# Turnings and scores side by side in the attention stages of a two-block transformer on one core

## The chip, the cores and the metric

The kernel runs on 1 core of one Trainium2 chip. The time is what the device takes for one launch, in microseconds; the median of 3 runs before the change is 2911.08 us (2909.06 to 2913.7). The profile is of one further execution.

## The reference

Two blocks work on 512 tokens of width 1024, all in float32. The first block has two layers, each with a feed-forward part, a "mix" part (a convolution beside an attention with forget gates), a cross-attention to a memory and a second feed-forward part. The second block has a differential attention layer and a "stick-breaking" attention layer. The change touches the three self-attentions:

```
# mix: 8 heads of 64, causal
s = q k^T * scale + c_q - c_k ;  p = softmax(where(mask, s, -inf)) ;  o = p v
# differential: 8 heads, each with two q, k pairs of 64 and one v of 128
a = softmax(q1 k1^T * scale) - lam * softmax(q2 k2^T * scale) ;  o = a v
# stick-breaking (last stage): 16 heads of 64
z = q k^T * scale ;  log_1mb = where(mask, log_sigmoid(-z), 0)
suffix = reverse_cumsum(log_1mb) - log_1mb
a = where(mask, exp(log_sigmoid(z) + suffix), 0) ;  o = a v
```

## The kernel before, in words

**Stages and products.** The program has ten stages in a row (`STAGES`): ffn1, mix, x, ffn2 twice, then diff and sb (the last stage). TensorE computes every projection as a float32 product in three matmuls of high and low halves (`mm3`, L1525 to L1527): low weight times high input, high times low, high times high. In the text one such matmul of 512 columns is called **a product**; a projection tile has 24 of them (8 blocks of the width, 3 matmuls each). Weights come by DMA into RAW. ScalarE copies the high half to WH (L1872, L1875 for weights with a gain), VectorE subtracts to get the low half WL (L2255). In the last stage GpSimd first multiplies the raw weights by a gain (L2783).

**A row.** The attention works on pairs of heads. A pair t has four rows of 128 queries, numbered n = 4t to 4t+3; row i of a pair sees 128, 256, 384 or 512 keys. A row passes through these steps:

- **scores** (`pair_scores`, L1770): six matmuls of 64 rows of the array, into PSUM banks 4 and 5. In the mix two more of 40 rows (L1785) add the forget term.
- **weights of the row.** In mix and diff VectorE masks (L2423, L2617) and takes the maximum (L2425, L2619), ScalarE takes the exponential with its sum (L2003, L2129), then VectorE and in the mix GpSimd scale the row. In the last stage ScalarE takes two sigmoids (L2170, L2171), VectorE scans the products along the keys (L2701) and corrects the diagonal (L2705), and GpSimd multiplies the two (L2889).
- **turning** (`turn`, L1531): TensorE transposes blocks of 128 by 128 into bank 6 (diff) or banks 6 and 7 (mix, last). One row takes i+1 transposes in diff and 2(i+1) in the other two. ScalarE copies the high half out (L2139, L2179) and VectorE takes the low half (L2644, L2711), which frees the banks for the next turning.
- **values** (`bpv`, L1811 and L1812 in mix and last): after four turned rows, products with v.

**What sets the order.** The class `Plan` writes one list of steps, and each engine works through the entries that concern it, strictly in that order, with waits on semaphores. The attention of four rows is a side stream (`att`) that is woven into the main stream of projection matmuls (`weave`). Each `yield` in `att` ends one step. `stream(g, rate)` says how many steps are taken per unit of main work; two units are one `mm3` of 512 columns, so three products. A turning belongs to row n-2 (mix, diff) or n-3 (last) and stands in `att` just before the scores of row n, with a `yield` after each. Steps that follow up on another engine are put off with `later(k, ...)` by k units of main work, and `due(...)` puts them into the list at once where something needs them. The slots of WH and WL and a clock of planned steps (`PACE`) decide where in the list the low halves of the weights (`low`) stand.

**Groups in the last stage.** For t = 2 to 7 the loop in `stick` weaves four rows into the q and k tiles of the next pair. For odd t a value tile is added. So groups alternate: long ones (80 units of main work) and short ones (48).

**Other steps that the text names.** `gb` (L2723) multiplies the gate, which frees the gate's bank; `gy` (L2730) applies the gate to the output; `gl` (L2736) takes the output's low half. In diff `dn` (L1726) sums squares of q or k with 8 small matmuls and waits for two passes on ScalarE (`dsq`, L2097 and L2102); `dlo` (L2608) writes the low half of q or k; `dol` (L2669) writes the low half of the output.

Of the kernel before, what the change touches and what calls it, by code (L numbers as in the profile page):

```python
# [108 lines left out]
class Plan:  # L109
# [372 lines left out]
    def mix(self, s):  # L482
# [15 lines left out]
        def qk(w, t):  # L498
            b = self.take()
            yield from self.tile(((s, f"{w}{t}"), 0), b)  # L500
            self.give(b, "bql", (s, w, t))
            self.heads_in(s, w, t)
# [22 lines left out]
        def values_of(t, hh):  # L525
            b = self.take()
            self.bank_of[s, t, hh] = b
            self.add("mpv", (s, t, hh), "pv", "pvx")
            self.give(b, "mpl", (s, t, hh))
            self.later(3, "mps", (s, t, hh), "pvs")  # L530
            self.later(6, "mpq", (s, t, hh), "ysq", *(("yacc",) if t and hh else ()), "yh")
            self.later(10, "mpl", (s, t, hh), "yl")

        def att(n0, n1):

            for n in range(n0, n1):
                m = n - 2
                if m > 0 and m % 4 == 0:
                    self.due("btl", (s, m - 1))
                    for i in range(2):  # L540
                        self.due("evl", (((s, f"v{(m - 4) // 8}"), 0), i))
                    for hh in range(2):
                        values_of(m // 4 - 1, hh)
                        yield
                if 0 <= m < 16:
                    self.due("mn", (s, m))
                    self.due("btl", (s, m - 1))
                    self.later(4, "btl", (s, m), "pl")
                    self.add("bt", (s, m), "ptr", "ph")
                    yield  # L550
                if n < 16:
                    for w in "qk":
                        self.due("bql", (s, w, n // 4))
                    self.due("mn", (s, n - 1))
                    self.add("ms", (s, n), "score", "nbias", "exps")
                    self.later(10, "mn", (s, n), "fac", "gprob")
                    yield
# [44 lines left out]
        self.drain(self.flow(self.values(s, 0)))  # L602
        self.drain(self.flow(conv("c", 0)))
        self.add("ctr", (s,), "ctr", "cq")
        side = self.stream(att(0, 4), 6.5 / 64)
        self.weave(self.flow(self.chain(conv("v", 0), conv("b", 0), qk("q", 1), qk("k", 1))), side)
        for m in (1, 2):
            self.finish(side)
            side = self.stream(att(4 * m, 4 * m + 4), 10.5 / 80)
            self.weave(self.flow(self.chain(conv("c", m), conv("v", m), conv("b", m), qk("q", m + 1), qk("k", m + 1))), side)  # L610
        self.finish(side)
        side = self.stream(att(12, 16), 10.5 / 80)
        self.weave(self.flow(self.chain(self.values(s, 1), conv("c", 3), conv("v", 3), conv("b", 3))), side)
        self.finish(side)
        self.own_banks(0, 1, 2, 3, 4, 5)
# [1 line left out]
        side = self.stream(att(16, 19), 4.5 / 44)  # L617
# [178 lines left out]
    def diff(self, s):  # L796
# [52 lines left out]
        def att(n0, n1):  # L849

            for n in range(n0, n1):
                m = n - 2
                if m > 0 and m % 4 == 0:
                    self.due("dtl", (s, m - 1))
                    for i in range(2):
                        self.due("evl", (((s, f"v{(m - 4) // 8}"), 0), i))
                    values_of(m // 4 - 1)
                    yield
                if 0 <= m < 32:
                    self.due("dc", (s, m))  # L860
                    self.due("dtl", (s, m - 1))
                    self.add("dt", (s, m), "ptr", "ph")
                    self.later(4, "dtl", (s, m), "pl")
                    yield
                if n < 32:
                    for w in "qk":
                        self.due("dlo", (w, n // 4))
                    self.due("dc", (s, n - 1))
                    self.add("ds", (s, n), "score", "nbias", "exps")
                    self.later(6, "dc", (s, n), "prob")  # L870
                    yield
# [33 lines left out]
        for t in range(7):  # L905
            main = [qk("k", t + 1), qk("q", t + 1)]
            if t in (2, 4):
                main.append(self.values(s, t // 2 + 1))
            main.append(gated(t))
            side = self.stream(att(4 * t, 4 * t + 4), 9.4 / (80 if t in (2, 4) else 48))  # L910
            self.weave(self.flow(self.chain(*main)), side)
            self.finish(side)
        out = []
# [15 lines left out]
            for c, b in ((0, 6), (1, self.take())):  # L929
                yield from self.tile(out[2], b, c, range(7))  # L930

        side = self.stream(att(28, 33), 10.4 / 33)
        self.weave(self.flow(opening()), side)
        self.finish(side)
        side = self.stream(att(33, 36), 2.4 / 28)
# [116 lines left out]
    def stick(self, s):  # L1052
# [37 lines left out]
        def att(n0, n1):  # L1090

            for n in range(n0, n1):
                m = n - 3
                if m > 0 and m % 4 == 0:
                    self.due("btl", (s, m - 1))
                    for i in range(2):
                        self.due("evl", (((s, f"v{(m - 4) // 8}"), 0), i))
                    for hh in range(2):
                        values_of(m // 4 - 1, hh)
                        yield  # L1100
                if 0 <= m < 32:
                    self.due("bmul", (s, m))
                    self.due("btl", (s, m - 1))
                    self.add("bt", (s, m), "ptr", "ph")
                    self.later(5, "btl", (s, m), "pl")
                    yield
                if n < 32:
                    for w in "qk":
                        self.due("bql", (s, w, n // 4))
                    self.due("bmul", (s, n - 1))  # L1110
                    self.add("bs", (s, n), "score", "exps", "sbe")
                    self.later(5, "bsc", (s, n), "fac", "bel")
                    self.later(5, "bmul", (s, n), "gprob")
                    yield
# [15 lines left out]
        self.add("mq", (s,), "mask", "zero", "tri")  # L1130
        for w, t in (("q", 0), ("k", 0), ("q", 1)):
            self.heads_in(s, w, t)
        side = self.stream(att(0, 4), 6 / 64)
        self.weave(self.flow(self.chain(qk("k", 1), self.values(s, 0), gated(0))), side)
        for t in range(2, 8):
            self.finish(side)
            main = [qk("q", t), qk("k", t)]
            if t % 2:
                main.append(self.values(s, t // 2))
            if t < 7:  # L1140
                main.append(gated(t - 1))
            side = self.stream(att(4 * t - 4, 4 * t), 10.5 / (32 + (32 if t % 2 else 0) + (16 if t < 7 else 0)))
            self.weave(self.flow(self.chain(*main)), side)
        self.finish(side)
        banks = (0, 4, 6, 2)
# [4 lines left out]
            yield from self.chain(gated(6), gated(7))  # L1150
            yield from self.mm(out[0], range(0, 6))

        side = self.stream(att(28, 33), 13 / 56)
        self.weave(self.flow(opening()), side)
        self.finish(side)
        side = self.stream(att(33, 36), 6 / 20)
# [1767 lines left out]
```

## Time and profile before

| | |
|---|---|
| runs | 2909.06, 2911.08, 2913.7 us |
| the profiled execution | 2911.05 us, of it the span of instructions 2909.2 us |
| TensorE matmul busy | 2843.3 us (98%) |
| TensorE weight load busy | 2363.5 us (81%) |
| VectorE busy | 1676.3 us (58%) |
| ScalarE busy | 1092.2 us (38%) |
| GpSimd busy | 397.3 us (14%) |
| mean granted TensorE clock | 0.995 |
| chain of work that ended last | TensorE 82%, VectorE 10%, ScalarE 3%, issue 3% |

Matmuls overlap: one of 512 columns is shown with 0.39 us, and the next one starts 0.23 us after it. So the busy share of TensorE says little of how much time could be won; the starts of matmuls, one behind the other, say it. A number in square brackets at the end of a row is how long the engine sat idle before it, and who ended that.

### The profile page before, as it was taken

The page shows a single profiled execution, that of the slowest core. Times are in us where ns is not written, and L with a number is a line of the kernel's source. Part 1 is how long each engine was busy: PE and PEld are TensorE (multiplying, and loading weights), DVE is VectorE, ACT ScalarE, POOL GpSimd, SP SyncE. Part 2 cuts the span into 40 slices and gives each one's busy share as a digit, 9 for nine tenths or more (in the row PEclk, how much of TensorE's full clock was granted, in tenths as well). Part 3 has the DMA queues.
Part 4 walks back from the last instruction along what each step waited for, and adds up shares of the span by engine and source line. Part 5 has one row for each costly group of instructions (what it writes and reads, how often), then busy time and mean ns, then how long its engine had stood idle before and what let it go on. Part 6 is the DMA issues. An engine that isn't in the chain of part 4 may idle for free.

```text
span 2909.2 us, 34967 instructions
## 1 busy us (share of the span) xinstructions
PE 2843.3 (98%) x14241; PEld 2363.5 (81%) x14241; DVE 1676.3 (58%) x2400; ACT 1092.2 (38%) x1699; POOL 397.3 (14%) x263
## 2 busy tenths in 40 slices
PE   8999999999999999999999999999999899899988
PEld 7888887888888888888887889888888787678777
DVE  5554357675464533555247776555533677768884
ACT  4322244554332322323234454422222444444442
POOL 2000111110100001000011220100001322154430
PEclk9999999999999999999999999999999999999999
DMA  4332332243233233332323233233323222131211
GB/s 141 101 95 94 95 88 73 66 127 106 87 94 97 88 101 98 101 95 87 105 71 92 68 108 118 80 109 95 101 91 98 70 64 69 47 88 59 72 59 51
DMA packets 302240, 258.08 MB, mean 89 GB/s; under 512 B 11367, under 2 KB 299904, under 8 KB 302080
## 3 DMA queue, kind: packets, MB, share of 16 engines
q1 hardware_dynamic: 300704, 254.76, 28.7%
q8 instruction: 113, 1.85, 0.3%
q10 hardware_dynamic: 1024, 1.05, 0.2%
q14 instruction: 47, 0.39, 0.0%
q0 software_dynamic: 352, 0.03, 0.0%
HBM read 252.66 MB, written 2.10 MB: 88 GB/s over the span
## 4 chain that ended last, share of the span: by engine, by line
PE 82%; DVE 10%; ACT 3%; issue 3%; POOL 2%; DMA 1%; ACTq 0%; SPq 0%; POOLq 0%; DVEq 0%
PE PS L1525 26%; PE PS L1527 25%; PE PS L1526 25%; DVE WL L2255 3%; PE PS L1531 2%; PE PS L1770 1%; DVE AF L2701 1%; DVE SM L2619 1%; ACT AF L2129 0%; PE PS L1623 0%; PE PS L1812 0%; PE PS L1811 0%; DVE AR L2711 0%; ACT WH L1872 0%; POOL SM L2869 0%
## 5 line engine op out<-in xcount | busy, mean ns | idle before, releaser
L2255 DVE TENSOR_TENSOR WL<-RAW,WH 128x1024 fp32r<-128x1024 f32 x480 | 617.9, 1293 | 572.9 <-ACT WH L1872 572.6
L1525 PE MATMUL PS<-XH,WL 128*128 128x512 f32 x2256 | 904.4, 401 | 2.9 <-DVE XL L2265 2.9
L1527 PE MATMUL PS<-XH,WH 128*128 128x512 f32 x2256 | 883.3, 392 | 0.0
L1526 PE MATMUL PS<-XL,WH 128*128 128x512 f32 x2256 | 882.1, 391 | 0.0
L1872 ACT ACTIVATE WH<-RAW 128x1024 fp32r<-128x1024 f32 x448 | 465.4, 1044 | 1005.9 <-PE PS L1527 994.6
L1525 PEld LDWEIGHTS PS<-XH,WL 128*128 128x128 f32 x2256 | 425.8, 189 | 101.5 <-issue 12.7
L1527 PEld LDWEIGHTS PS<-XH,WH 128*128 128x128 f32 x2256 | 425.2, 188 | 91.5
L1526 PEld LDWEIGHTS PS<-XL,WH 128*128 128x128 f32 x2256 | 426.3, 189 | 81.1
L1525 PE MATMUL PS<-AR,WL 128*128 128x512 f32 (+1 forms) x1216 | 465.3, 383 | 7.3 <-DVE SC L2599 3.5
L1527 PE MATMUL PS<-AR,WH 128*128 128x512 f32 (+1 forms) x1216 | 460.7, 379 | 0.0
L1526 PE MATMUL PS<-AR,WH 128*128 128x512 f32 (+1 forms) x1216 | 460.6, 379 | 0.0
L2805 POOL TENSOR_TENSOR SC<-SC 128x512 f32<-128x512 f32 x70 | 117.5, 1678 | 1619.3 <-ACT SC L1897 1614.7
L1525 PEld LDWEIGHTS PS<-AR,WL 128*128 128x128 f32 x1216 | 229.4, 189 | 52.0 <-issue 9.2
L1527 PEld LDWEIGHTS PS<-AR,WH 128*128 128x128 f32 x1216 | 229.2, 188 | 43.1
L1526 PEld LDWEIGHTS PS<-AR,WH 128*128 128x128 f32 x1216 | 229.4, 189 | 41.0
L1525 PE MATMUL PS<-WH,XL 128*128 128x256 f32 x384 | 113.3, 295 | 0.8 <-DVE AR L2693 0.8
L2324 DVE TENSOR_TENSOR AF<-PS,RB 128x512 f32<-128x512 f32 x88 | 60.4, 687 | 85.9 <-PE PS L1527 85.9
L1526 PE MATMUL PS<-WL,XH 128*128 128x256 f32 x384 | 109.1, 284 | 0.0
L1527 PE MATMUL PS<-WH,XH 128*128 128x256 f32 x384 | 109.0, 284 | 0.0
L2337 DVE TENSOR_TENSOR AR<-AF,AR 128x512 fp32r<-128x512 f32 x88 | 60.9, 692 | 61.7 <-ACT AR L1934 61.7
L2318 DVE TENSOR_TENSOR SC<-PS,RB 128x512 f32<-128x512 f32 x88 | 60.1, 687 | 59.1 <-PE PS L1527 45.6
L1934 ACT ACTIVATE AR<-AF 128x512 fp32r<-128x512 f32 x88 | 55.3, 628 | 98.5 <-DVE AF L2332 98.5
(259 smaller groups left out, 3000.0 us busy)
## 6 DMA issues: line engine op xcount, KB each, us to landing
RAW<-in_w_ffn_gu_dram SPq DMA_DIRECT2D x176, 512.0 KB, 3.5
RAW<-in_w_ffn_down_dram SPq DMA_DIRECT2D x80, 512.0 KB, 3.4
RAW<-in_w_mix_in_dram SPq DMA_DIRECT2D x48, 512.0 KB, 4.0
RAW<-in_w_xkv_dram SPq DMA_DIRECT2D x32, 512.0 KB, 3.4
RAW<-in_a_w_in_dram SPq DMA_DIRECT2D x32, 512.0 KB, 4.2
RAW<-in_w_mix_out_dram SPq DMA_DIRECT2D x16, 512.0 KB, 3.4
RAW<-in_w_xq_dram SPq DMA_DIRECT2D x16, 512.0 KB, 4.1
RAW<-in_w_xo_dram SPq DMA_DIRECT2D x16, 512.0 KB, 3.4
```

The lines of the kernel that those rows point to most:

```text
L1525: pe.matmul(o, ll, rh, start=start, stop=False, skip_group_check=skip)
L1526: pe.matmul(o, lh, rl, start=False, stop=False, skip_group_check=skip)
L1527: return pe.matmul(o, lh, rh, start=False, stop=stop, skip_group_check=skip)
L1531: t = pe.transpose(PS[b][:, i * 128:(i + 1) * 128], src[:, i * 128:(i + 1) * 128], ID)
L1770: w = pe.matmul(PS[4 + hh][:, 0:N], QK[r, q, qs], QK[r, k, 0:N], start=q == sl + 1, stop=last and q == sl and k == sl + 2)
L1872: act.activation(h, src, ACT.Copy).then_inc(sg["wh"].up(n))
L1934: act.activation(AH[:, f, :], AF[:, (f % 2) * T:(f % 2) * T + T], ACT.Copy).then_inc(sg["fh"].up(s, f))
L2255: dve.tensor_tensor(l, raw_slot(n), F(h), ALU.subtract).then_inc(sg["wl"].up(n))
L2318: dve.tensor_tensor(S[f % 2], PS[C.banks[f % 2]][:, :], RB[:, :], ALU.mult).then_inc(sg["fs"].up(s, f))
L2324: dve.tensor_tensor(w, PS[C.banks[f % 2]][:, :], RB[:, :], ALU.mult).then_inc(sg["fu"].up(s, f))
L2337: dve.tensor_tensor(AL[:, f, :], AF[:, (f % 2) * T:(f % 2) * T + T], F(AH[:, f, :]), ALU.subtract).then_inc(sg["fl"].up(s, f))
L2805: pool.tensor_tensor(S[5], S[5], square_of(m), ALU.add).then_inc(sg["acc"].up(s, m))
```

## The change

In the three `att` functions the `yield` between a turning and the scores of the later row is kept only where no scores follow (n of 16 or 32 and above). Everywhere else the two now form one step. A group of four rows had 10 steps (8 of rows, 2 of values; 9 in diff) and now has 6 (5 in diff), so the rates are lowered in step: the step with both is longer apart from the next. No instruction is added or taken away; TensorE has 12921 rows of program in both.

```diff
@@ in mix, att (the same in diff and stick with 32)
                     self.later(4, "btl", (s, m), "pl")
                     self.add("bt", (s, m), "ptr", "ph")
-                    yield
+                    if n >= 16:
+                        yield
@@ mix
-        side = self.stream(att(0, 4), 6.5 / 64)
+        side = self.stream(att(0, 4), 4.3 / 64)
...
-            side = self.stream(att(4 * m, 4 * m + 4), 10.5 / 80)
+            side = self.stream(att(4 * m, 4 * m + 4), 6.3 / 80)
@@ diff
-            side = self.stream(att(4 * t, 4 * t + 4), 9.4 / (80 if t in (2, 4) else 48))
+            side = self.stream(att(4 * t, 4 * t + 4), 5.3 / (80 if t in (2, 4) else 48))
...
-        side = self.stream(att(28, 33), 10.4 / 33)
+        side = self.stream(att(28, 33), 6.3 / 33)
@@ stick
-        side = self.stream(att(0, 4), 6 / 64)
+        side = self.stream(att(0, 4), 4.3 / 64)
...
-            side = self.stream(att(4 * t - 4, 4 * t), 10.5 / (32 + (32 if t % 2 else 0) + (16 if t < 7 else 0)))
+            side = self.stream(att(4 * t - 4, 4 * t), 6.3 / (32 + (32 if t % 2 else 0) + (16 if t < 7 else 0)))
...
-        side = self.stream(att(28, 33), 13 / 56)
+        side = self.stream(att(28, 33), 8.2 / 56)
```

Line numbers of the changed kernel are higher by 3 in what follows (L1531 is L1534, L2711 is L2714).

**Place 1, last stage, start of a short group.** TensorE before: the first row's scores of the pair (128 columns), six products, the third row's turning, and nine products up to the next scores.

```order
L1770 MATMUL PS<-AR 128x128 x6
L1525 MATMUL PS<-XH,WL 128x512
L1526 MATMUL PS<-XL,WH 128x512
L1527 MATMUL PS<-XH,WH 128x512
L1525 MATMUL PS<-XH,WL 128x512
L1526 MATMUL PS<-XL,WH 128x512
L1527 MATMUL PS<-XH,WH 128x512
L1531 MATMUL PS<-IDR,SC 128x128 x6
L1525 MATMUL PS<-XH,WL 128x512
```

TensorE now, at the same turning:

```order
L1529 MATMUL PS<-XL,WH 128x512
L1530 MATMUL PS<-XH,WH 128x512
L1534 MATMUL PS<-IDR,SC 128x128 x6
L1773 MATMUL PS<-AR 128x256 x6
L1528 MATMUL PS<-XH,WL 128x512
L1529 MATMUL PS<-XL,WH 128x512
```

The second row's scores moved up behind the third row's turning. Counted over the whole list, that turning stands 3 products later than before, and the scores of the fourth row before it (512 columns) stand where they stood: 27 products now lie between the two, where 24 lay.

VectorE at that place, from the gate's product `gy` to the low half of the second row's turning (L2711 with 256 columns), which frees banks 6 and 7 for the third row. Before:

```order
L2730 TENSOR_TENSOR AF<-AF,PS 64x512 x2
L2736 TENSOR_TENSOR AR<-AF,AR 128x512
L2392 SCALAR_TENSOR_TENSOR AR<-PS,SM,AR 128x2x64 x4
L2255 TENSOR_TENSOR WL<-RAW,WH 128x1024 x2
L2711 TENSOR_TENSOR AR<-PS,AR 128x2x128
L2718 TENSOR_TENSOR AF<-PS,RB 128x512
L2701 SCALAR_TENSOR_TENSOR AF<-AF,AR 128x512 x2
L2705 TENSOR_TENSOR SC<-SC,AR 128x2x128
L2723 TENSOR_TENSOR AF<-AF,PS 128x512
L2255 TENSOR_TENSOR WL<-RAW,WH 128x1024
L2711 TENSOR_TENSOR AR<-PS,AR 128x2x256
```

Now:

```order
L2733 TENSOR_TENSOR AF<-AF,PS 64x512 x2
L2395 SCALAR_TENSOR_TENSOR AR<-PS,SM,AR 128x2x64 x4
L2258 TENSOR_TENSOR WL<-RAW,WH 128x1024 x2
L2739 TENSOR_TENSOR AR<-AF,AR 128x512
L2721 TENSOR_TENSOR AF<-PS,RB 128x512
L2714 TENSOR_TENSOR AR<-PS,AR 128x2x128
L2704 SCALAR_TENSOR_TENSOR AF<-AF,AR 128x512 x2
L2708 TENSOR_TENSOR SC<-SC,AR 128x2x128
L2726 TENSOR_TENSOR AF<-AF,PS 128x512
L2258 TENSOR_TENSOR WL<-RAW,WH 128x1024
L2714 TENSOR_TENSOR AR<-PS,AR 128x2x256
```

The low half of the output (L2736) moved behind the low halves of the values (L2392) and of the weights; from the scan on the rows are the same.

**Place 2, diff, ScalarE at the start of the stage.** Between the exponential of the third row (L2129, 384 columns) and that of the fourth (512), before:

```order
L2129 ACTIVATE AF,SM<-PS,SM 128x384 x2
L2139 ACTIVATE AR<-PS 128x2x128
L1872 ACTIVATE WH<-RAW 128x1024
L2129 ACTIVATE AF,SM<-PS,SM 128x512 x2
L2097 ACTIVATE SC<-PS 128x512
L2102 ACTIVATE SC<-PS,SM 128x512
L2119 ACTIVATE AR<-SC 128x512
```

Now:

```order
L2132 ACTIVATE AF,SM<-PS,SM 128x384 x2
L1875 ACTIVATE WH<-RAW 128x1024
L2100 ACTIVATE SC<-PS 128x512
L2105 ACTIVATE SC<-PS,SM 128x512
L2122 ACTIVATE AR<-SC 128x512
L2115 DMA AR<-SC 8x512
L2116 DMA AR<-SC 8x512
L2115 DMA AR<-SC 8x512
L2116 DMA AR<-SC 8x512
L2142 ACTIVATE AR<-PS 128x2x128
L2132 ACTIVATE AF,SM<-PS,SM 128x512 x2
```

The two passes (L2097, L2102) for which `dn` waits on TensorE moved ahead of the fourth row's exponential.

**Place 3, last stage, VectorE at the last gate.** The `gb` (L2723) frees the bank for the second values product of the pair (`bpv`, L1811); the L2471 around it belong to the two values products. Before:

```order
L2705 TENSOR_TENSOR SC<-SC,AR 128x2x128
L2255 TENSOR_TENSOR WL<-RAW,WH 128x1024
L2718 TENSOR_TENSOR AF<-PS,RB 128x512
L2255 TENSOR_TENSOR WL<-RAW,WH 128x1024
L2471 TENSOR_TENSOR PS<-PS,AR 64x512
L2723 TENSOR_TENSOR AF<-AF,PS 128x512
L2471 TENSOR_TENSOR PS<-PS,AR 64x512
```

Now:

```order
L2708 TENSOR_TENSOR SC<-SC,AR 128x2x128
L2474 TENSOR_TENSOR PS<-PS,AR 64x512
L2721 TENSOR_TENSOR AF<-PS,RB 128x512
L2726 TENSOR_TENSOR AF<-AF,PS 128x512
L2258 TENSOR_TENSOR WL<-RAW,WH 128x1024
L2474 TENSOR_TENSOR PS<-PS,AR 64x512
```

Two subtractions of weights (L2255) no longer stand between the scan and the gate.

## Rows read from the trace of the kernel before

**Rows 1.** Stretches: length; busy of PE, PEld, DVE, ACT, POOL; PEclk; DMA share, GB/s.

```profile
2270.00:2595.00 325.00, 303.65 (x1692) 246.01 (x1692) 236.78 (x476) 146.48 (x305) 86.21 (x54) 0.98 0.22 65
2595.00:2909.00 314.00, 290.36 (x1628) 237.41 (x1628) 232.45 (x302) 136.08 (x202) 111.29 (x61) 0.98 0.21 64
```

**Rows 2.** Timeline of TensorE (start, us, engine, line): side by side, then apart.

```profile
2305.70 0.66 PE L1531 MATMUL PS<-IDR,SC 128*128 128x128 f32 x4
2306.28 0.97 PE L1770 MATMUL PS<-AR 64*128 64x512 f32 x6
2307.18 0.50 PE L1525 MATMUL PS<-XH,WL 128*128 128x512 f32 x1
...
2652.04 0.40 PE L1527 MATMUL PS<-XH,WH 128*128 128x512 f32 x1
2652.36 0.98 PE L1770 MATMUL PS<-AR 64*128 64x512 f32 x6
2653.27 0.50 PE L1525 MATMUL PS<-XH,WL 128*128 128x512 f32 x1
...
2656.82 0.60 PE L1531 MATMUL PS<-IDR,SC 128*128 128x128 f32 x4
2657.17 0.48 PE L1525 MATMUL PS<-XH,WL 128*128 128x512 f32 x1
2657.49 0.39 PE L1526 MATMUL PS<-XL,WH 128*128 128x512 f32 x1
```

**Rows 3.** Waits of TensorE from 2440 us on: us in total, times, longest.

```profile
PE PS L1531 <- DVE AR L2711: 14.0, 7, 2.9
```

**Rows 4.** Short stretches, columns as in rows 1; the clock is PEclk.

```profile
576.00:584.00 8.00, 7.21 (x40) 5.78 (x39) 6.55 (x11) 6.63 (x11) 1.98 (x2) 1.00 0.26 73
2313.00:2317.00 4.00, 3.75 (x16) 3.17 (x17) 1.85 (x6) 0.71 (x2) 1.29 (x1) 0.72 0.50 150
2488.00:2492.00 4.00, 3.89 (x17) 3.17 (x18) 3.09 (x6) 0.80 (x4) 0.00 (x0) 0.61 0.25 75
2700.00:2704.00 4.00, 3.43 (x12) 3.01 (x13) 4.00 (x4) 1.41 (x2) 3.55 (x2) 0.57 0.42 135
2831.00:2835.00 4.00, 3.15 (x20) 2.44 (x21) 4.00 (x7) 1.95 (x3) 2.94 (x2) 1.00 0.84 256
```

**Rows 5.** Timeline of TensorE at place 1: fourth row's scores, third row's turning.

```profile
2690.26 0.97 PE L1770 MATMUL PS<-AR 64*128 64x512 f32 x6
...
2700.57 1.51 PE L1531 MATMUL PS<-IDR,SC 128*128 128x128 f32 x6 [2.52 <-DVE AR L2711]
```

**Rows 6.** Timeline of VectorE at place 1.

```profile
2688.61 0.69 DVE L2736 TENSOR_TENSOR AR<-AF,AR 128x512 fp32r<-128x512 f32 x1 [1.65 <-ACT AR L2187]
...
2696.74 3.09 DVE L2255 TENSOR_TENSOR WL<-RAW,WH 128x1024 fp32r<-128x1024 f32 x1
...
2704.78 0.95 DVE L2711 TENSOR_TENSOR AR<-PS,AR 128x768 fp32r<-128x768 f32 x1
```

**Rows 7.** Timeline at place 2: ScalarE, then TensorE.

```profile
2312.50 0.69 ACT L2102 ACTIVATE SC<-PS,SM 128x512 f32<-128x512 f32 x1
...
2313.25 1.05 PE L1726 MATMUL PS<-SM,SC 128*128 128x2 f32 x8 [3.05 <-ACT SC L2102]
```

**Rows 8.** Timeline of VectorE and TensorE in diff, a later head.

```profile
2480.18 0.69 DVE L2669 TENSOR_TENSOR AR<-SC,AR 128x512 fp32r<-128x512 f32 x1
...
2481.38 0.42 DVE L2644 TENSOR_TENSOR AR<-PS,AR 128x256 fp32r<-128x256 f32 x1
...
2488.11 0.55 PE L1770 MATMUL PS<-AR 64*128 64x128 f32 x6 [2.26 <-DVE AR L2608]
```

**Rows 9.** Timeline at place 3: VectorE, then TensorE.

```profile
2843.93 1.97 DVE L2255 TENSOR_TENSOR WL<-RAW,WH 128x1024 fp32r<-128x1024 f32 x1
...
2847.27 0.80 PE L1811 MATMUL PS<-AR 128*128 128x512 f32 x1 [3.08 <-DVE AF L2723]
```

**Rows 10.** Timeline of TensorE at the end of the first mix attention.

```profile
559.85 1.06 PE L1531 MATMUL PS<-IDR,SC 128*128 128x128 f32 x8 [1.32 <-DVE AR L2711]
```

More of the change, by code:

```diff
@@ L608, in mix @@
             self.finish(side)
-            side = self.stream(att(4 * m, 4 * m + 4), 10.5 / 80)
+            side = self.stream(att(4 * m, 4 * m + 4), 6.3 / 80)
             self.weave(self.flow(self.chain(conv("c", m), conv("v", m), conv("b", m), qk("q", m + 1), qk("k", m + 1))), side)
         self.finish(side)
-        side = self.stream(att(12, 16), 10.5 / 80)
+        side = self.stream(att(12, 16), 6.3 / 80)
         self.weave(self.flow(self.chain(self.values(s, 1), conv("c", 3), conv("v", 3), conv("b", 3))), side)
@@ L863, in att @@
                     self.later(4, "dtl", (s, m), "pl")
-                    yield
+                    if n >= 32:
+                        yield
                 if n < 32:
@@ L1105, in att @@
                     self.later(5, "btl", (s, m), "pl")
-                    yield
+                    if n >= 32:
+                        yield
                 if n < 32:
```

## The prediction, made before the changed kernel was run

> **What bounds the kernel now.** I read the busy time by stretches first, then the list of waits of TensorE, then its timeline around the turnings and scores, and last the timelines of the engines that it waited for. In diff and in the last stage TensorE runs matmuls for 303.65 of 325 us and for 290.36 of 314 us; VectorE is next with 236.78 and 232.45 us [rows 1]. So TensorE sets the time, and what can be won is what stands between its matmuls: a switch of the array's form, a wait, or a lower clock.
>
> The waits are few and long. From 2440 us on seven turnings waited 14.0 us for L2711, which frees banks 6 and 7 from the turning before [rows 3]. A long wait also costs afterwards. After the wait of 2.52 us at 2700.57 [rows 5] the granted clock over 4 us is 0.57 instead of 1.00 [rows 4]: TensorE went from 2.4 to 1.2 GHz for most of them, which loses 4 x 0.43 = 1.7 us. After the 2.26 us at 2488.11 [rows 8] it is 0.61, after the 3.05 us at 2313.25 [rows 7] it is 0.72; they lose 1.6 and 1.1 us. At 2831, where a turning waited too, it stayed at 1.00 [rows 4]. So I price a wait of above 2.2 us at its length plus 1.1 to 1.7 us, and a shorter one at its length.
>
> **The change part by part.** I sum against the profiled execution, 2911.05 us, which is 1.85 us above its span; the median of the runs is 2911.08, so the same sum holds for both.
>
> *Side by side or apart.* In the mixes 28 turnings get scores right behind them (14 in each), in diff 30, in the last stage 29: 87 pairs. Apart, a turning of four blocks takes 0.35 us to the next product (2656.82 to 2657.17), and that product 0.32 to the following one, where 0.23 is usual: 0.09 more. A product ahead of scores takes 0.32 (2652.04 to 2652.36), again 0.09 more, and the scores of 512 columns take 0.91. Together 0.35 + 0.09 + 0.09 + 0.91 = 1.44 us. One pair already stands side by side: 2305.70 to 2307.18, 1.48 us [rows 2]. So the switch is paid once more wherever the scores go, and the pair wins nothing: 87 x 0.04 is 3.5 us more at one end, and if one of the two 0.09 were saved, 87 x 0.09 = 7.8 us less at the other. I take 0, nearest to the pair that is there: its turning had itself waited shortly, which explains the 0.04.
>
> *Place 1, the third row's turning at the start of short groups* (two of them, at 2700.57 and one 67 us later). From the fourth row's scores to this turning it takes 2700.57 - 2690.26 = 10.3 us, the last 2.52 of them waiting [rows 5]. The turning now stands 3 products later, 0.7 us. VectorE sat idle for 1.65 us ahead of L2736 [rows 6]; in the new order the low halves of values and weights fill that, but the second values product before it stands 4.5 products (1.0 us) later, so the chain comes some 0.6 us sooner. The wait shrinks to 2.52 - 0.7 - 0.6 = 1.2 us, and the clock should stay up. That is 1.3 + 1.4 (the mean of 1.1 and 1.7) = 2.7 us, twice 5.4. What is late next: VectorE now does a subtraction of weights ahead of the fourth turning's low half (L2711, 512 columns), which the first values product needs. Where GpSimd works at the same time such a subtraction takes 3.09 us [rows 6]. The third turning's low half ended 2704.78 + 0.95 - 2700.57 = 5.2 us after the turning began, so VectorE has little in hand there. Between 0 and 3.1 us each; I take half, 1.6, twice 3.2. Place 1 in sum: -2.2.
>
> The Trainium skill ("SBUF — State Buffer", section "Who interferes with whom") says that a VectorE instruction with two inputs from SBUF contends with a GpSimd instruction that reads SBUF. The trace agrees, with 3.09 us for the L2255 that lies beside GpSimd's multiplication. By that rule alone no order of VectorE's work makes the pair of them cheaper, so all of place 1 could only move; that is a rival below.
>
> *The long groups* keep their wait: there the turning also comes 3 products later (0.7 us), but a multiplication by the norm (L2687, as long as L2736's 0.69 in [rows 6]) is now ahead of L2711. Nothing.
>
> *Place 2, diff's first pair.* TensorE waited 3.05 us in `dn` for L2102, which ended at 2313.19 because the two passes stood behind the fourth row's exponential [rows 7]. They are now ahead of it. The wait goes, and with it 1.1 us of low clock: 4.15; I take 4.0. What is late next: in the long groups (two in diff) the same two passes now stand behind the first row's exponential, with 12 products (2.7 us) from its scores to `dn`. From nothing to the 4.15 of this place each; I take 0.6, twice 1.2. The cover is those 12 products. In the short groups the fourth row's scores follow the third's after 12 products, where 15 stood: 0.7 us less for mask, maximum and exponential. From 0 to 0.7 at four heads; I take half: 1.4.
>
> *Diff, first scores of a late head* waited 2.26 us for `dlo` [rows 8]. Mask and maximum of the row before now stand ahead of `dol` and `dtl` (0.69 and 0.42, less their overlap: 1.0 us sooner), and the scores come 3 products earlier (0.7). The wait is 2.26 - 1.0 + 0.7 = 1.9 us, just under what lowered the clock: 0.3 + 1.6 = 1.9 us won. At the other end nothing. Diff in sum: -4.0 + 1.2 + 1.4 - 1.9 = -3.3.
>
> *Place 3.* The second values product waited 3.08 us for `gb`; ahead of it VectorE did two subtractions of weights, one of 1.97 us [rows 9]. Both moved out of the way. The gate still needs the first values product, its copy and two passes, so I leave 1.1 us: 2.0 won, and 1.7 of clock. -3.7; at worst nothing.
>
> *Mixes.* The turning before the last values waits 1.32 us for L2711 [rows 10]. The second row's turning moved down to the fourth row's scores, so its low half and copy fall into the stretch ahead of that wait: one VectorE instruction of that kind takes 0.7 to 0.95 [rows 6]. I take +0.7 in each of two stages, 1.4; between 0 and twice 0.95.
>
> Sum: -2.2 - 3.3 - 3.7 + 1.4 = -7.8, so 2911.05 - 7.8 = 2903.3; I say 2903.5.
>
> **The rivals.**
>
> *The waits only move (no change).* For: VectorE does the same work in order, and its load of 232 in 314 us [rows 1] comes in bursts; a turning that waits less reaches the next one sooner. Then place 1 and the head in diff win nothing (+2.2, +1.9) and place 3 only its length less the new waits (+1.7): -7.8 + 5.8 = -2, 2909. Against: place 2 is a wait that the order alone made.
>
> *Late low halves (slower).* One mechanism: VectorE and ScalarE now have long entries ahead of what TensorE waits for, a subtraction of weights ahead of L2711 in short groups and the first row's exponential ahead of L2102 in long ones. It decides from 2.2 us on, as then the clock falls too. Then each of the two long groups in diff costs 4.15 instead of 0.6 (+7.1), each values product of place 1 3.1 instead of 1.6 with its own clock loss (+3.0 + 2.8): -7.8 + 12.9 = +5.1, 2916. For: 3.09 us for one subtraction. Against: 12 products of cover.
>
> *All low clocks go (much faster).* The last stage has other long waits of the kind of [rows 3]. If three more fall under 2.2 us with 0.7 us of wait and 1.7 of clock each, that is 7.2 more: 2896.
>
> *Turnings do not keep the clock up (slower).* Eight blocks and six scores now stand together in 13 places of mix and last. If each such clump lowered the clock once, as a long wait does, 13 x 1.7 = 22 us: 2925 with the rest. Against: the stretch that holds the memory's sixteen turnings together has 1.00 [rows 4]. The Trainium skill ("TensorE: Matmul & The Clock Gate", section "Part 4: PE-mode transpose") says that a transpose does not count as busy for the clock; this row doesn't show it.
>
> **How the numbers follow.** Forecast 0.50, with an own range of 2898 to 2908; waits only move 0.24; late low halves 0.14; all low clocks go 0.10; clump clock 0.02. What can be told from no change is 0.2%, 5.8 us, so faster ends at 2905.2. Four fifths of the forecast (0.40), nearly all of the much faster (0.10) give 0.50 faster. The other fifth of the forecast (0.10) and the moving waits (0.24) give 0.34 same. Slower: 0.14 + 0.02 = 0.16. The range reaches down to 2894, a little below the much faster case, and up to 2914, to which the moving waits scatter; above it lies most of the slower cases, some 0.13.
>
> **What would show it.** In the changed profile: the pairs take 1.48 us and the busy shares of all engines stay. At place 2 `dn` waits less than 0.5 us. The third turning of short groups waits about 1.2 us with a clock of 1.00 after it. The second values product at the end waits about 1 us. The granted clock falls in five fewer places, so its mean rises. It is wrong if `dn` in the long groups or the values products wait over 2 us, if the clock falls as often as before, or if a pair takes under 1.4 us: then the switch was worth something after all.

## The result, and the profile after

| | before | after |
|---|---|---|
| time, median of 6 runs | 2910.85 us (2908.96 to 2913.70) | 2921.38 us (2916.78 to 2924.98) |
| ratio, 95% interval | | 1.0033 (1.0021 to 1.0045) |
| profiled execution, span | 2911.05, 2909.2 us | 2919.01, 2917.2 us |

The change made the kernel 9.6 us slower (0.0033 x 2911); forecast were 2903.5 us, and 2914 as the upper end. The two profiled executions differ by 8.0 us. The loss stands in one stage. The timeline has a mark that both kernels share, the sums over ones that open a norm (L1623 before, L1626 after); the last stage is counted up to 4.0 us before the end of the span, in every run. From mark to mark the mixes take 237.4 and 236.9 us before, 235.5 and 235.0 after. Diff goes from 324.6 to 341.5 us, the last stage from 309.8 to 305.2. So 3.8 us are won in the mixes, 4.6 in the last stage, and 16.9 lost in diff, 8.5 more in sum; the other stages are 0.5 us shorter.

The same columns as in [rows 1], cut at the marks: of the kernel before, diff and last stage,

```profile
2270.80:2595.40 324.60, 303.61 (x1692) 245.98 (x1693) 235.98 (x476) 145.68 (x304) 85.90 (x54) 0.98 0.23 65
2595.40:2905.20 309.80, 290.09 (x1628) 237.38 (x1628) 231.90 (x302) 135.48 (x201) 110.89 (x60) 0.98 0.21 62
```

and of the kernel after:

```profile
2266.50:2608.00 341.50, 308.82 (x1692) 252.70 (x1692) 243.99 (x476) 147.67 (x304) 86.70 (x54) 0.96 0.21 62
2608.00:2913.20 305.20, 286.49 (x1627) 235.69 (x1628) 235.27 (x302) 133.64 (x201) 108.29 (x60) 0.99 0.21 63
```

Length less TensorE's busy time is its idle time: in diff 21.0 us before and 32.7 after, 11.7 more. The other 5.2 us are the same matmuls taking longer, with a mean granted clock of 0.96. In the last stage the idle time hardly moved (19.7 to 18.7 us); 3.6 of its 4.6 us are faster matmuls. VectorE, with the same 476 instructions, is busy for 8.0 us more in diff.

Some names that follow: `dc` is VectorE's scaling of a row (a reciprocal, two instructions on one column, a multiply-add). `don` is TensorE's sum over ones of the squares of a head's output; it writes bank 7. `dom` is VectorE's gating of that output. The first scores of a head are those of its first row (128 columns); before them TensorE needs the low halves of the head's q and k. I call a head late when its first scores wait for these.

What TensorE waited for in diff, the kernel before and then after (us in total, times, longest; the largest rows of each):

```profile
PE PS L1726 <- ACT SC L2102: 6.0, 5, 3.1
PE PS L1531 <- DVE SC L2657: 4.0, 3, 1.5
PE PS L1525 <- DVE SC L2599: 3.5, 1, 3.5
PE PS L1770 <- DVE AR L2608: 2.7, 3, 2.3
```

```profile
PE PS L1773 <- DVE AR L2611: 6.0, 4, 2.9
PE PS L1729 <- ACT SC L2105: 5.2, 5, 1.2
PE PS L1528 <- DVE SC L2602: 4.2, 1, 4.2
PE PS L1626 <- DVE SC L2606: 3.9, 4, 1.3
PE PS L1534 <- DVE AR L2647: 3.9, 3, 2.2
PE PS L1528 <- DVE AR L2647: 3.4, 3, 1.4
```

Before, eleven waits of over 0.6 us made up most of the sum; after, there are twenty-five, many of about 1 us: at a head's first scores for its low half (L2611), at `dn` for the squares (L2105), and at the values products and turnings for a turned row's low half (L2647).

**The long groups.** ScalarE's timeline at the squares of a k, before and after:

```profile
2352.81 0.59 ACT L2097 ACTIVATE SC<-PS 128x512 f32<-128x512 f32 x1
2353.28 0.70 ACT L2102 ACTIVATE SC<-PS,GB 128x512 f32<-128x512 f32 x1
2355.54 0.46 ACT L2129 ACTIVATE AF<-PS,SM 128x128 f32<-128x128 f32 x1 [1.56 <-DVE SM L2624]
```

```profile
2352.30 0.46 ACT L2132 ACTIVATE AF<-PS,SM 128x128 f32<-128x128 f32 x1 [2.16 <-DVE SM L2627]
2352.75 0.45 ACT L2132 ACTIVATE AF<-PS,SM 128x128 f32<-128x128 f32 x1
2353.19 0.59 ACT L2100 ACTIVATE SC<-PS 128x512 f32<-128x512 f32 x1
2353.66 0.69 ACT L2105 ACTIVATE SC<-PS,GB 128x512 f32<-128x512 f32 x1
```

The exponential now stands first, ScalarE sits idle for 2.16 us for it, and the squares can't pass. TensorE then waits for them, and ahead of that for the head's low half:

```profile
2349.68 0.55 PE L1773 MATMUL PS<-AR 64*128 64x128 f32 x6 [0.74 <-DVE AR L2611]
2354.41 1.05 PE L1729 MATMUL PS<-SM,SC 128*128 128x2 f32 x8 [1.22 <-ACT SC L2105]
```

The clock fell behind both squares of this group, though neither wait reaches 2.2 us, from which my rule counted. The other long group has the same two waits, 1.25 and 1.05 us (at 2428.86 and 2437.96), and there the clock stayed up (third row). The fourth row is of the last stage, around a turning's wait of 0.93 us at 2721.34:

```profile
2356.00:2360.00 4.00, 4.00 (x14) 3.04 (x13) 1.13 (x2) 0.00 (x0) 2.90 (x2) 0.57 0.27 80
2366.00:2370.00 4.00, 4.00 (x23) 4.00 (x23) 2.20 (x7) 0.00 (x0) 2.27 (x2) 0.57 0.41 116
2428.00:2444.00 16.00, 14.08 (x102) 12.89 (x103) 8.89 (x22) 5.73 (x12) 5.85 (x4) 1.00 0.33 96
2719.00:2723.00 4.00, 3.07 (x21) 2.13 (x19) 3.97 (x6) 2.02 (x4) 2.49 (x3) 1.00 0.00 0
```

**VectorE beside GpSimd.** Where most of the 8.0 us more come from, in the timeline after:

```profile
2340.81 1.28 POOL L2878 TENSOR_TENSOR SC<-SC,AF 128x512 f32<-128x512 f32 x1
2340.83 1.28 DVE L2639 SCALAR_TENSOR_TENSOR SM<-SM 128x1 f32<-128x1 f32 x1
...
2348.84 0.69 DVE L2611 TENSOR_TENSOR AR<-SC,AR 128x512 fp32r<-128x512 f32 x1 [0.24 <-ACT AR L2122]
```

An instruction of `dc` on one column takes 1.28 us and ends with GpSimd's multiplication by the cosine. Before it took 0.22 us, and ended 1.4 us ahead of it:

```profile
2343.73 0.22 DVE L2636 SCALAR_TENSOR_TENSOR SM<-SM 128x1 f32<-128x1 f32 x1
2345.31 1.66 POOL L2875 TENSOR_TENSOR SC<-SC,AF 128x512 f32<-128x512 f32 x1
```

It is no single case. All 32 instructions of this line (ns: shortest, median, longest), before and after:

```profile
L2636 DVE SCALAR_TENSOR_TENSOR SM<-SM x32: 218/219/223, 2296.2 to 2542.1; 128x1 f32<-128x1 f32 x32
```

```profile
L2639 DVE SCALAR_TENSOR_TENSOR SM<-SM x32: 219/220/1282, 2294.4 to 2551.6; 128x1 f32<-128x1 f32 x32
```

Five of the 32 take 1.25 to 1.28 us, each starting 0.02 to 0.06 us behind a multiplication of GpSimd's; together they take 5.3 us more than before. Two multiply-adds of `dc` took 1.87 and 1.48 us instead of 0.75 and 0.48, and the sixteen multiplications by the sine take 2.0 us more in sum. Other lines take less (copies 2.2 us). Three of the five stand 9 us ahead of a late head's first scores, which then waited 0.74, 0.77 and 1.53 us. The cause is in the order. The `dn` of VectorE (one instruction that takes over TensorE's sums, L2583 after) starts a power on GpSimd (1.64 us), and the multiplication follows it. Before, `dc` stood directly behind that `dn`; now the two instructions of `dom` and the turned row's low half stand between (from 2339.05 to 2340.64 in the timeline after, 1.6 us; VectorE's `dn` is at 2338.96), so that `dc` meets the multiplication's start. The Trainium skill ("SBUF — State Buffer", section "Who interferes with whom") calls the shared ports "an exclusive lock": that the short instruction lasts just as long as GpSimd's agrees with it.

### The profile page after: what moved, and what is told of

Read it like the earlier page. It is cut to its first block, busy times and chain, and to the rows that moved or that the text cites. A ratio compares the mean times of both kernels' runs of the same rounds, so it can differ in the third digit from the quotient of the medians.

```text
span 2917.2 us, 34969 instructions
## 1 busy us (share of the span) xinstructions
PE 2842.8 (97%) x14241; PEld 2369.7 (81%) x14241; DVE 1689.5 (58%) x2400; ACT 1092.6 (37%) x1699; POOL 395.4 (14%) x263
## 3 DMA queue, kind: packets, MB, share of 16 engines
q10 hardware_dynamic: 1024, 1.05, 0.2%
## 4 chain that ended last, share of the span: by engine, by line
PE 86%; DVE 7%; ACT 2%; issue 2%; POOL 1%; DMA 0%; ACTq 0%; SPq 0%; POOLq 0%; DVEq 0%
PE PS L1528 27%; PE PS L1530 26%; PE PS L1529 26%; DVE WL L2258 2%; PE PS L1773 2%; PE PS L1534 1%; DVE AF L2704 1%; PE PS L1815 1%; PE PS L1626 1%; PE PS L1814 1%; DVE AR L2714 1%; DVE SM L2622 1%; ACT AF L2132 0%; ACT WH L1875 0%; POOL SC L2816 0%
## 5 line engine op out<-in xcount | busy, mean ns | idle before, releaser
L2258 DVE TENSOR_TENSOR WL<-RAW,WH 128x1024 fp32r<-128x1024 f32 x480 | 624.5, 1307 | 574.7 <-ACT WH L1875 574.3
```

The costliest lines, as they stand in the source:

```text
L2258: dve.tensor_tensor(l, raw_slot(n), F(h), ALU.subtract).then_inc(sg["wl"].up(n))
```

## The experiments

Each ran in 5 rounds beside the kernel before. Stage lengths are from mark to mark in one profiled execution each; idle is length less TensorE's busy time; the clock is the mean granted one. In e7, e9 and e12 GpSimd multiplies one column of 512, so their output is not the reference's.

| run | ratio to before (95%) | diff us | idle in it | clock in it | last us |
|---|---|---|---|---|---|
| before | 1 | 324.6 | 21.0 | 0.98 | 309.8 |
| the change | 1.0033 (1.0021 to 1.0045) | 341.5 | 32.7 | 0.96 | 305.2 |
| e1 mixes and last | 0.9972 (0.9963 to 0.9981) | 327.0 | 20.6 | 0.97 | 306.8 |
| e2 diff | 1.0060 (1.0047 to 1.0072) | 342.4 | 33.9 | 0.97 | 311.3 |
| e3 turnings moved | 1.0030 (1.0018 to 1.0042) | 345.1 | 30.8 | 0.94 | 305.0 |
| e4 scores moved | 1.0061 (1.0048 to 1.0075) | 353.7 | 37.3 | 0.94 | 305.4 |
| e5 by hand | 1.0049 (1.0037 to 1.0062) | 350.2 | 31.4 | 0.93 | 303.8 |
| e6 long groups later | 0.9996 (0.9988 to 1.0005) | 334.5 | 27.8 | 0.97 | 305.3 |
| e7 GpSimd one column | 0.9981 (0.9972 to 0.9990) | 329.0 | 27.4 | 0.98 | 303.8 |
| e8 first group | 0.9964 (0.9952 to 0.9977) | 325.5 | 21.9 | 0.98 | 306.9 |
| e9 control | 0.9957 (0.9945 to 0.9970) | 322.3 | 17.5 | 0.97 | 305.8 |
| e10 cosine on VectorE | 1.0015 (1.0006 to 1.0024) | 340.2 | 29.9 | 0.95 | 305.3 |
| e11 the same, first group | 0.9971 (0.9959 to 0.9982) | 326.7 | 22.5 | 0.97 | 305.3 |
| e12 e6 and e7 | 0.9962 (0.9948 to 0.9976) | 325.0 | 21.7 | 0.98 | 304.8 |

**Which stage: e1 and e2.** e1 keeps the `yield` in diff and its old rates, e2 has only diff's part of the change:

```
                     self.later(4, "dtl", (s, m), "pl")
-                    if n >= 32:
-                        yield
+                    yield
-            side = self.stream(att(4 * t, 4 * t + 4), 5.3 / (80 if t in (2, 4) else 48))
+            side = self.stream(att(4 * t, 4 * t + 4), 9.4 / (80 if t in (2, 4) else 48))
```

> The two mixes and the last stage as in the changed kernel, diff as in the kernel before. Theory A (the loss is diff's alone, and the stages add up): the profiled runs show the mixes 4.2 us and the last stage 4.6 us shorter, so 2910.9 - 8.8 = 2902, and diff takes the 324.6 us of before between the first sums of its norm and those of the last stage. Theory B (the last stage only gains because diff left its buffers or its clock in another state): the last stage takes its 309.0 us of before again, 2906 to 2907.

> Diff alone as in the changed kernel, mixes and last stage as before. Theory A (stages add up): diff costs 16.9 us, 2910.9 + 16.9 = 2928, and the mixes and the last stage stand as before. Theory B (part of the loss comes from what the mix leaves behind): under 2922.

Measured -8.1 and +17.5 us; their sum, +9.4, is the change's +9.6. The stages add up, and diff alone loses. A caution comes with e1: its diff, in the old order, takes 327.0 us and not 324.6, with the same idle time. Equal waits cost different amounts of clock, so one profile of diff is good to some 2.5 us. e2 shows the same. Its diff has the order of the change and nearly its waits (25 of over 0.6 us as well, 34.5 us in sum against 34.0), but the clock fell at other places: at 2433 and 2443 behind the squares of the second long group, where the change has 1.00, and not behind those of the first (1.00 from 2358 to 2375).

**Which places: e3 and e4.** The old rate, with an empty step ahead of each pair (e3) or behind it (e4):

```
+                if 0 <= m < 30:          # e3, ahead of the turning
+                    yield
...
+                    if m >= 0:           # e4, behind the scores
+                        yield
```

> As the changed kernel, but in diff every pair stands where the scores stood before: only the turnings move, 7.5 matmuls of 512 columns later. Theory A (diff loses by the new places of the scores: ahead of a late q or k's squares in long groups, and earlier than a late head's low halves are ready): the waits for the norm of q and k in long groups (1.2 and 1.1 us) and of a late head's first scores (0.75 to 2.9 us) go back to before; diff takes 324 to 329 us, in all 2902 to 2907. Theory B (turning and scores side by side are themselves the load: copy, low half, mask and maximum come in one burst): diff keeps most of the 16.9 us, 2915 to 2921. Theory C (GpSimd's multiplication beside VectorE's short instructions, 1.28 us instead of 0.22 in five places): 5 us stay, 2907.

> As the changed kernel, but in diff every pair stands where the turnings stood before: only the scores move, 7.5 matmuls of 512 columns earlier. Theory A (the places of the scores): a late head's first scores now stand at 12 fewer matmuls behind its low halves' inputs than before, 2.7 us each at seven heads, so diff takes 340 us or more, 2919 to 2930, worse than with the pairs at the scores' places by over 10 us. Theory B (the burst): the same as with the pairs at the scores' places within 4 us. Theory C: the five long short-instructions appear here as well.

Theory A failed for e3: with every score in its old place diff still took 345.1 us. Theory C failed as well: none of the 32 short instructions is long here (nor in e4 and e5). The waits moved:

```profile
PE PS L1530 <- DVE AR L2649: 14.0, 7, 3.3
```

Seven values products waited for the fourth row's low half. Its turning now stood only 6 products ahead of them in short groups and 12 in long ones (matmuls of 256 columns counted half), where before there were 15 and 25.5. In e4 four turnings waited 2.3 us each and first scores up to 4.39. So no single place is to blame: a turning has a deadline behind it (the values), scores have one ahead (their low halves), and a pair must meet both. By its total e3 fits theory B (the burst) too. Against B stands e4: the same pairs at other places, and diff 8.6 us longer, where B allowed 4 and theory A asked for over 10.

**Places by hand: e5.** The steps stand at written-out places; the code that reads them is left out here.

```
...
+            side = self.stream(att(4 * t, 4 * t + 4, (18, 34, 50, 60, 76) if t in (2, 4) else (11, 18, 31, 36, 46) if t else (6, 11, 20, 34)), 1)
...
```

> As the changed kernel, but in diff the steps of the rows stand at places written out (in pairs of 512-column matmul counts of 1.5: short groups 11, 18, values 31, 36, 46; long groups 18, 34, values 50, 60, 76; first group 6, 11, 20, 34), chosen so that a pair stands right behind the squares of a q or k and not ahead of them, the fourth row's turning stands 19 matmuls ahead of the values and a late head's first scores 3 matmuls later. Theory A (each place has its own deadline, and the loss is that of missed deadlines): the waits for the norm of q and k in the long groups, the two of the values (1.45 us each) and the three of late first scores (0.74, 0.77, 1.53) go; diff takes 325 to 330 us instead of 341.5, in all 2903 to 2908. Theory B (with pairs no places suit, since a burst of two rows' work delays whatever comes next): 335 us or more, 2913 or more.

Theory A missed: 350.2 us, in theory B's range. Nearly all waits aimed at went (`dn` 0.7 us in sum, the values none for a low half; 1.53 became 1.30), but six sums over ones in `don` waited 14.2 us. Four of them waited for bank 7, which a multiplication of k on VectorE frees, and two for the squares of the output, which now stood behind another entry on ScalarE:

```profile
PE PS L1637 <- DVE SC L2617: 7.2, 4, 2.2
PE PS L1637 <- ACT SC L2159: 7.0, 2, 3.5
```

**The squares: e6.**

```
-            side = self.stream(att(4 * t, 4 * t + 4), 5.3 / (80 if t in (2, 4) else 48))
+            side = self.stream(att(4 * t, 4 * t + 4), (4.9 / 80 if t in (2, 4) else 5.3 / 48))
```

> As the changed kernel, but in diff's two long groups the steps stand some 2 to 6 matmuls later (4.9 instead of 5.3 steps over the group), so that the first two pairs stand right behind the squares of k and q instead of right ahead of them. Theory A (ScalarE's exponential ahead of the squares is what the norm waits for): four waits (1.22, 1.05, 1.25, 1.05 us) and two falls of the clock by 1.6 us go, 7.8 us, 2921.4 - 7.8 = 2913 to 2914. Theory B (the waits move to the later low halves): within 2 us of the changed kernel, 2920 to 2923.

As theory A has it: diff 7.0 us shorter (4.9 of it idle time, 2.1 faster matmuls), the ratio lower by 0.0037 (10.8 us, give or take 4 by the two intervals). `dn` no longer waits in the long groups:

```profile
2354.83 0.95 PE L1729 MATMUL PS<-SM,SC 128*128 128x2 f32 x8
...
2362.83 0.95 PE L1729 MATMUL PS<-SM,SC 128*128 128x2 f32 x8
```

**GpSimd: e7 and its control e9.** e7 is the change, e9 is e1, both with

```
-                pool.tensor_tensor(z, z, COS, ALU.mult).then_inc(sg["dco"].up(w, t))
+                pool.tensor_tensor(z[:, 0:1], z[:, 0:1], COS[:, 0:1], ALU.mult).then_inc(sg["dco"].up(w, t))
```

> As the changed kernel, but GpSimd's sixteen multiplications by the cosine in diff work on one column instead of 512 (the output is then not the reference's; VectorE, ScalarE and TensorE have all their work). Theory C (VectorE's one-element instruction of 1.28 us instead of 0.22, five times, and one multiply-add of 1.87 instead of 0.75, come from GpSimd's multiplication beside them, and delay a late head's low halves): they are back to 0.22 and 0.75, the waits of 0.74, 0.77 and 1.53 us at first scores shrink by 0.7 to 1.1 us each and that of 2.92 us by about 1.1 and with a fall of the clock: 4 to 7 us less than the changed kernel, 2914 to 2917. Theory D (hidden behind other things): at most 1 us.

> Control for the run with GpSimd's one column: mixes and last stage as changed, diff in the order of before, GpSimd's sixteen multiplications by the cosine on one column (output not the reference's). Theory C1 (the new order put VectorE's short instructions beside GpSimd's multiplication, the old one didn't): diff stays within 3 us of the 327.0 and 325.5 us of its order of before, in all 2902 to 2906. Theory C2 (GpSimd's multiplication costs the old order as much): diff 315 us, in all 2893 or less, and then the run with one column said nothing on the change.

All 32 short instructions are back at 0.22 us in e7, and the waits at 2317 and 2349 went from 2.92 to 1.48 and from 0.74 to nothing. The wait of 1.53 us stayed, against theory C:

```profile
L2639 DVE SCALAR_TENSOR_TENSOR SM<-SM x32: 218/219/222, 2291.3 to 2537.1; 128x1 f32<-128x1 f32 x32
```

Diff is 12.5 us shorter, more than expected; 7.2 of that are faster matmuls. In the old order the same edit wins 4.7 us (a shorter path for everybody), a bit over C1's bound. What the new order pays for GpSimd is the difference: 7.8 us by the profiles, 10.8 by the ratios (0.0052 less 0.0015), give or take 6 by the four intervals. So that there is a cost is shown, its size only roughly. Of the 7.8 us only 2.3 are idle time and 5.5 are clock: in e7 the four squares of the long groups still wait 1.02 to 1.05 us, but behind the first two the clock now stays at 1.00 (2348 to 2366).

**Both causes: e12**, the edits of e6 and e7 together.

> The changed kernel with diff's long groups 2 to 6 matmuls later and GpSimd's cosine on one column (output not the reference's): the two edits that took 7.0 and 12.5 us from diff. Theory (two causes of their own: exponentials ahead of the squares, and stretching beside GpSimd): diff 341.5 - 7.0 - 12.5 = 322 us, or somewhat more where both took away the same fall of the clock, 322 to 326; in all 2897 to 2902. Rival (both edits only happened to shift the same waits): 328 us or more, 2905.

As expected: diff takes 325.0 us, 2.7 more than the control e9 with the same edit in the old order (by ratio 1.5 us, within error). So the two causes account for 341.5 - 327.0 - 2.7 = 11.8 of the 14.5 us between the change and e1; by the ratios, for 16.3 of 17.8. They overlap: alone, they take 7.0 and 7.8 (14.8). This also speaks against theory B of e5, since here pairs stand in all of diff and nearly reach the old order, if only with GpSimd's work cut. The edit of e6 has no control in the old order.

**Can the cost be avoided: e10 and e11.** The cosine moves to VectorE, in the change and in e8.

```
                 dve.tensor_tensor(z, F(SWAP), SIN, ALU.mult).then_inc(sg["dsn"].up(w, t))
+                c = S["qk".index(w)]
+                dve.tensor_tensor(c, c, COS, ALU.mult).then_inc(sg["dco"].up(w, t))
...
-                pool.tensor_tensor(z, z, COS, ALU.mult).then_inc(sg["dco"].up(w, t))
```

> The changed kernel, but the sixteen multiplications by the cosine in diff are done by VectorE behind its own of the sine, and GpSimd has none. Theory C: no VectorE instruction lies beside one of GpSimd's 512 columns any more; VectorE gets 16 x 0.69 = 11.0 us of work and loses 5.2 + 2.1 + 2.0 us of stretching; the waits of 0.74, 0.77 and part of 1.53 and 2.92 us go: diff 331 to 336 us, in all 2909 to 2915. Rival (VectorE's own 0.69 us ahead of the sums delays a late head's low halves as much as the stretching did): diff 339 us or more, 2918 or more.

> As the kernel with only diff's first group in pairs (2902.3 us), with the cosine on VectorE as well. Theory C: there little is stretched, so VectorE's 11 us are pure load: within 3 us of 2902, more likely above. Rival: the waits of 1.95 and 2.27 us for a late head's low halves shrink by the 1.1 us that VectorE's multiplication is shorter than GpSimd's: 2898 to 2900.

e10 is undecided. Its ratio gives back 5.2 us of the change's loss, but the profiled diff only 1.3. The stretched instructions are gone, two first scores wait 0.32 us instead of 0.74 and 0.77, and that at 2316 still 2.69. Of the 2.8 us of idle time won, slower matmuls (clock 0.95) took back 1.5. e11 is no better than e8, as theory C had it.

**Place 2 alone: e8.** Only diff's first group gets pairs; the best version that does all the work.

```
-                    if n >= 32:
+                    if n >= 4:
                         yield
-            side = self.stream(att(4 * t, 4 * t + 4), 5.3 / (80 if t in (2, 4) else 48))
+            side = self.stream(att(4 * t, 4 * t + 4), (9.4 if t else 5.3) / (80 if t in (2, 4) else 48))
```

> Mixes and last stage as changed; in diff only the first group of four rows has its turnings and scores side by side, the others stand as before. As the prediction had it (the norm's wait of 3.05 us and 1.1 us of clock go): 4 us less than with diff as before, 2905.9 - 4 = 2902. Theory A (the wait comes back at the next row's scores, 1.29 us, and at the second head's first scores, 2.92 us, since what was put ahead now holds back those): within 1.5 us of 2906.

2902.33 us, 0.9964: 10.5 us faster than the kernel before. Against e1 it is 2.3 us by ratio and 1.5 in the stage, between the two theories; the two intervals overlap. `dn` at place 2 waits no more, but the scores around it do: 1.11, 1.28 and 1.95 us.

## Why the prediction was wrong

**What bounds it:** right. TensorE's idle time and clock explain both the loss and the gains.

**A pair costs nothing:** right. In the first mix (wait-free ones) a turning of four blocks costs 0.44 us beyond the products' usual spacing of 0.23 (at 433.71) and scores of eight matmuls 1.33 (at 437.59); together they cost 1.78 (at 435.58 after). And the changed order's clumps did not lower the clock in mixes or last stage.

**Place 1:** right for what it priced. The third row's turning of a short group waited 1.40 us (said: 1.2, [rows 5] had 2.52), the values product 1.33 (said: 1.6), the clock stayed at 1.00:

```profile
2716.03 0.84 PE L1534 MATMUL PS<-IDR,SC 128*128 128x128 f32 x6 [1.40 <-DVE AR L2714]
2721.34 1.06 PE L1534 MATMUL PS<-IDR,SC 128*128 128x128 f32 x8 [0.93 <-DVE AR L2714]
2727.39 0.50 PE L1814 MATMUL PS<-AR 128*128 128x512 f32 x1 [1.33 <-DVE AR L2714]
```

**Place 3:** right in size. The 3.08 us of [rows 9] became 1.06, as said; the first values product, which had not waited, now waits 0.97.

**The last stage in sum** won 4.6 us where places 1 and 3 were to win 5.9, nearly all of it clock: its waits are as long in sum as before, but in shorter pieces. That the two numbers lie so near is partly luck. "The long groups keep their wait" was wrong: their third rows' turnings waited 1.54, 1.66 and 2.90 us before, and now nothing, nothing and 0.68. And losses came that had no term: the stage's first short group, which had no wait before, got 1.40, 0.80 and 1.53 us, and in the other two the fourth row's turning now waits 0.93 and 0.94.

**Place 2:** half right. The wait of 3.05 us in [rows 7] went:

```profile
2300.14 0.79 PE L1773 MATMUL PS<-AR 64*128 64x384 f32 x6 [1.29 <-ACT AF L2132]
...
2306.88 1.05 PE L1729 MATMUL PS<-SM,SC 128*128 128x2 f32 x8
...
2317.43 0.55 PE L1773 MATMUL PS<-AR 64*128 64x128 f32 x6 [2.92 <-DVE AR L2611]
```

But 4.21 us came back around it (1.29 and 2.92), at scores that stand directly behind a turning. I had named the row whose chain was freed and not those whose chain was put behind.

**Diff as a whole:** the step that failed, -3.3 us forecast, +16.9 in the profile and +17.5 by e2. Three terms:

- "From nothing to the 4.15 of this place each; I take 0.6, twice 1.2." There are two squares in each long group, k's and q's, so four places and not two. They waited 1.22, 1.05, 1.25 and 1.05 us, 4.6 in sum, and the clock fell behind the first two; e6 puts the place at 7.0 us. It was my rival "late low halves" (+7.1), whose mechanism was right for diff while I gave it 0.14 and put its threshold at a single wait of 2.2 us. The trace before already spoke against that threshold: the wait at 2831.86, with a clock of 1.00 [rows 4], was 2.24 us, and one of 2.20 us at 2279.30 had 0.71 from 2279 to 2283.
- VectorE beside GpSimd: no term at all, although the prediction priced the same thing for one subtraction of the last stage (3.09 us). It is some 8 to 11 us, by e7 against e9. In diff I had not laid the moved instructions against GpSimd's.
- "The wait is 2.26 - 1.0 + 0.7 = 1.9 us [...] just under what lowered the clock." It was 1.53, with a wait of 1.05 at the turning ahead, and the clock fell (0.57 from 2496 to 2500). First scores of three other heads waited besides (2.92, 0.74, 0.77), which the forecast did not look at.

The price of a fall was too low in one place: the 1.1 us at 2313 comes from a stretch that ends inside the fall. From 2314 to 2320 the clock is 0.72, which loses 6 x 0.28 = 1.7 us, as at the other places.

The waits for values and `don` (1.4 and 0.9 us at several heads) had no term either. What of them makes up the 2.7 us that e12 leaves was not tried.

**The signs:** "the clock falls as often as before" was named as a sign of being wrong, and it came. Counted in stretches of 2 us from the start of diff to the end of the last stage, there are eight falls before (four in diff, four in the last stage) and eight after (seven and one), where five fewer were forecast.

**Mixes:** +1.4 forecast, -3.8 measured. In the first mix the turning of [rows 10] waits 0.88 us instead of 1.32, and waits of 0.49 (values) and 0.85 (the first product) are gone. In the second mix 1.92 became 0.90, and 0.48 is gone. With new waits of some 0.2 us this is 2.6 of the 3.8 us; the rest is not traced. I had moved a VectorE instruction into the stretch ahead of the turning, without taking out what leaves it. This is read from the trace; no run tests it alone, but e1, with the same mixes, shows the same waits there.

## What to carry to other kernels

When independent chains share in-order engines, price a reordering at every entry that the moved step now stands ahead of, on every engine, and count the places from the order: here two squares per group, eight heads, and one deadline on each side of a pair. A change that wins in one stage may lose in another with the same code; take it stage by stage (e8, with part of the change, wins 10.5 us; the whole cost 9.6). Lay each moved VectorE instruction against GpSimd's timeline, the shortest ones too.

## What the hardware showed that I had not expected

- A VectorE instruction on one column lasts 1.28 us instead of 0.22 when it starts 0.02 to 0.06 us behind GpSimd's multiplication of 512 columns, and ends with it.
- The clock fell to half behind waits of 1.22 and 1.05 us that stand 10 us apart (2356 and 2366, 0.57), and did not behind 1.25 and 1.05 us that stand 9 us apart (1.00 from 2428 to 2444), nor behind 1.40, 0.93 and 1.33 us within 12 us in the last stage (1.00 from 2719 to 2723, and no fall in its later groups). In e2, with the same order of diff, a wait of 2.92 us had none (1.00 from 2321 to 2330), where the change fell. The length of one wait does not decide it, and what does is not shown; my threshold of 2.2 us was drawn from too few places. The same order of diff, with the same idle time, had a mean clock of 0.98 once and 0.97 once.
